# Summing one more half vector on VectorE, in its pauses, in a two-layer encoder kernel

## The reference, cut to what matters

```python
cs = silu(c)                                    # one vector of 1024
for i in range(2):
    mod = cs @ w_mod[i] + b_mod[i]              # 6 vectors of 1024: shift, scale, gate, twice
    sh_m, sc_m, g_m, sh_f, sc_f, g_f = split(mod, 6)
    h = rmsnorm(x) * (1 + sc_m) + sh_m          # x is 256 x 1024
    if i == 0:                                  # q, kv, index q, index k, u, v = split(h @ w_in)
        a = sparse attention with 8 heads, 64 keys chosen for each query
        u, v = gelu(u), layernorm(gelu(v))
        b = u * (w_s @ v + b_s)                 # w_s block lower triangular, 128 x 128 per group
        y = concat(a, b) @ w_o
    else:
        y = four trailing window means, minus h, times a small matrix per group
    x = x + g_m * y
    h = rmsnorm(x) * (1 + sc_f) + sh_f
    x = x + g_f * (32 experts, 2 chosen per token; each 1024 -> 256 -> 1024, SwiGLU)
out = rmsnorm(x)
```

## Time and profile before

| | |
|---|---|
| median of 3 runs | 684.23 us (683.09 to 684.79) |
| profiled execution | 683.93 us; its span from first to last instruction 682.1 us |
| TensorE busy | 625.4 us, 92% of the span |
| VectorE, ScalarE, GpSimd busy | 358.6, 179.3, 62.2 us |
| moved | 269.63 MB, 395 GB/s over the span |

### The profile page before, as it was taken

The page is one execution under the profiler, slowest core; times in us unless marked ns, Lnnn a source line. Parts: engine busy times, 40 slices in busy tenths (PEclk is TensorE's granted clock), DMA queues, the critical chain, the costliest instruction groups (busy, mean ns, idle before and its releaser), DMA issues.

```text
span 682.1 us, 11449 instructions
## 1 busy us (share of the span) xinstructions
PE 625.4 (92%) x4226; PEld 376.8 (55%) x4226; DVE 358.6 (53%) x869; ACT 179.3 (26%) x370; POOL 62.2 (9%) x111
## 2 busy tenths in 40 slices
PE   2799999999999999999999989999999999999894
PEld 1497758446665455545554457666555554555442
DVE  2258988998454643344334465735444344433445
ACT  2023352013432232122212233342223112321213
POOL 5010408950000000000000000000000000000000
PEclk9899999999999999999999999999999999999998
DMA  8999987999999999999999999999999999999991
GB/s 324 358 382 395 379 302 259 408 417 415 386 411 421 420 421 422 422 421 420 422 421 422 409 399 412 420 420 420 420 421 420 422 421 422 423 422 420 422 398 69
DMA packets 51534, 269.63 MB, mean 395 GB/s; under 512 B 4112, under 2 KB 6224, under 8 KB 27440
## 3 DMA queue, kind: packets, MB, share of 16 engines
q1 hardware_dynamic: 50720, 268.22, 97.0%
q0 software_dynamic: 784, 1.01, 0.5%
HBM read 268.17 MB, written 1.05 MB: 395 GB/s over the span
## 4 chain that ended last, share of the span: by engine, by line
PE 67%; DMA 19%; DVE 11%; issue 1%; ACT 1%; SPq 0%; POOL 0%; DVEq 0%; POOLq 0%
PE bank L965 15%; PE bank L977 14%; PE bank L998 12%; DMA ring<-in_w_gate 11%; DMA ring<-in_w_mod 8%; PE bank L1024 7%; PE bank L687 4%; DVE gates L1445 3%; PE bank L930 2%; PE bank L771 2%; DVE hT L1763 2%; PE bank L600 1%; PE bank L985 1%; PE bank L1081 1%; PE bank L734 1%
## 5 line engine op out<-in xcount | busy, mean ns | idle before, releaser
L965 PE MATMUL bank<-ring,arena 128*64 128x256 f32 x1024 | 116.8, 380 | 2.6 <-DMA ring<-in_w_gate 2.6
L977 PE MATMUL bank<-ring,arena 128*64 128x256 f32 x1024 | 117.2, 381 | 0.0
L965 PEld LDWEIGHTS bank<-ring,arena 128*64 128x64 f32 x1024 | 75.4, 137 | 50.9 <-issue 20.4
L977 PEld LDWEIGHTS bank<-ring,arena 128*64 128x64 f32 x1024 | 72.3, 137 | 41.2 <-issue 8.6
L1763 DVE SCALAR_TENSOR_TENSOR hT<-hT,bank 128x256 f32<-128x256 f32 x32 | 19.2, 601 | 136.6 <-PE bank L977 136.6
L1292 ACT CAST xn_parts<-arena 128x512 fp32r<-128x512 f32 x64 | 39.6, 619 | 106.8 <-DVE arena L1788 106.8
L1788 DVE SCALAR_TENSOR_TENSOR arena<-bank,hT,gates 128x512 f32<-128x512 f32 x64 | 48.0, 750 | 36.7 <-PE bank L998 35.4
L1024 PE MATMUL bank<-xn_parts,sel 128*128 128x512 f32 x256 | 67.1, 405 | 0.0
L998 PE MATMUL bank<-dn_w,hT 128*64 128x512 f32 x256 | 58.5, 598 | 1.1 <-ACT gates L1102 1.1
L1024 PEld LDWEIGHTS bank<-xn_parts,sel 128*128 128x128 f32 x256 | 45.7, 188 | 20.9 <-issue 12.4
L998 PE MATMUL bank<-gates,arena 128*64 128x512 f32 x112 | 51.1, 598 | 0.0
(11 more groups left out here) (324 smaller groups left out, 762.2 us busy)
## 6 DMA issues: line engine op xcount, KB each, us to landing
ring<-in_w_gate SPq DMA_DIRECT2D x32, 2048.0 KB, 17.7
ring<-in_w_up SPq DMA_DIRECT2D x32, 2048.0 KB, 18.3
ring<-in_w_mod SPq DMA_DIRECT2D x20, 2048.0 KB, 17.6
dn_w<-in_w_down SPq DMA_DIRECT2D x16, 2048.0 KB, 17.7
xn<-in_w_down SPq DMA_DIRECT2D x14, 1024.0 KB, 17.0
gates<-in_w_down SPq DMA_DIRECT2D x14, 1024.0 KB, 19.2
ring<-in_w_in SPq DMA_DIRECT2D x2, 2048.0 KB, 22.9
dn_w<-in_w_mod SPq DMA_DIRECT2D x2, 2048.0 KB, 12.0
```

Source lines behind the costliest of these rows:

```text
L965: ins = pe.matmul(bank[2][h * WIN:(h + 1) * WIN, 0:FE], xw[:, b, h, k, :], w[:, h, 0, k, :], start=(k == 0), stop=(k == KT - 1))
L977: ins = pe.matmul(bank[3][h * WIN:(h + 1) * WIN, 0:FE], xw[:, b, h, k, :], w[:, h, 1, k, :], start=(k == 0), stop=(k == KT - 1))
```

## The change

It has these parts.

1. `m4a` is summed by VectorE, no longer by TensorE: one slab after the attention's `divide`, the others at three points of `gelu_v`; `m4b` then adds onto that sum.
2. The gelu's polynomial takes one instruction, since ScalarE's square now carries the factor. The normalization of v goes from VectorE to ScalarE (`ln_bias`), and so does VectorE's copy of the sums over values (`keep_heads`), for both token tiles; the counter `cat_dve` is gone.
3. Rooms: `m5a` goes to ATT, `m5b` to ring 1; `usq` moves from dn_w to the arena (where q stood). m5a is issued when all attention weights are turned and v's layernorm has its mean square (`ln_ms`); before, m5b waited there for `bT_ready` too.
4. The distances' absolute value and the zeroing in w_s go from VectorE to GpSimd, early; w_s is turned on TensorE before the indexer's scores, and copied by ScalarE in two parts.
5. `reduce((0, 4))` stands before the output projection, `reduce((0, 3))` before its second half (before, both stood inside the second half).
6. The last early half, `("mod", 3)`, comes as two transfers of 1 MB, and TensorE takes its first two slabs when the first has come. The transfer of c is issued behind x's first tile.

```diff
-        gtmp, usq = scratch[:, 2048:3072]..., scratch[:, 3072:4096].rearrange("p (t d) -> p t d", t=4)
+        gtmp, usq = scratch[:, 2048:3072]..., ar(2048, 1024, t=4)
...
-                 ... (m3a, 2), (m3b, 0), (m5a, 1), (n4b, 2), (m5b, ATT),
+                 ... (m3a, 2), (m3b, 0), (m5a, ATT), (n4b, 2), (m5b, 1),
...
-        by_dve = [m2a, m2b, m4b, m3a, m3b, n4b, m5a, m5b]
+        by_dve = [m2a, m2b, m4a, m4b, m3a, m3b, n4b, m5a, m5b]
...
+                    if plan[n] == LAST_MOD:
+                        sp.dma_start(mod_at(n)[:, 0:2], src[:, 0:2]).then_inc(S["last_mod"], 16)
+                        sp.dma_start(mod_at(n)[:, 2:4], src[:, 2:4]).then_inc(arrived, 16)
...
-                if slot_of(n) in (ARENA_A, ARENA_B) or plan[n] == m5b:
+                if plan[n] == m5a:
+                    sp.wait_ge(S["p_turned"], 6)
+                    sp.wait_ge(S["ln_ms"], 1)
+                if slot_of(n) in (ARENA_A, ARENA_B):
...
             turn_p(0)
             turn_p(1)
-            vector((0, 4), (0,))
             pe.wait_ge(S["v_kept"], 2)
...
             values(1)
-            pe.wait_ge(S["cat_act"], 2)
-            pe.wait_ge(S["cat_dve"], 2)
+            reduce((0, 4))
+            pe.wait_ge(S["cat_act"], 4)
...
             def keep_heads(t):                     # ScalarE
-                act.wait_ge(S["pv_done"], 2 * t + 1)
-                act.copy(catT[0:HD, 0:4, t * P:(t + 1) * P], bank[3][0:HD, :]...)
+                act.wait_ge(S["pv_done"], 2 * t + 2)
+                for b in range(2):
+                    at = slice(b * HD, (b + 1) * HD)
+                    act.copy(catT[at, 0:4, t * P:(t + 1) * P], bank[3 + b][at, :]...)
...
             def gelu_poly(sq, v, after):           # VectorE
-                done(ts(sq, sq, GELU_A, 1.0, ALU.mult, ALU.add))
-                tt(sq, sq, v, ALU.mult).then_inc(after, 1)
+                stt(sq, sq, 1.0, v, ALU.add, ALU.mult).then_inc(after, 1)
...
+            accumulate((0, 4), 0, (0,))
             gelu_v()
-            keep_heads(0)
+            accumulate((0, 4), 0, (3,))
             accumulate((0, 4), 1)
```

More of the change, by code:

```diff
@@ L181, in trunk @@
                  (m2a, 0), (m2b, 1), (n0a, 2), (("in", "q"), ATT), (("in", "v"), 3), (n0b, 0), (("in", "u"), 1),
-                 (("out", 0), EARLY_W), (m4a, 2), (m4b, 0), (("out", 1), 3), (m3a, 2), (m3b, 0), (m5a, 1), (n4b, 2), (m5b, ATT),
+                 (("out", 0), EARLY_W), (m4a, 2), (m4b, 0), (("out", 1), 3), (m3a, 2), (m3b, 0), (m5a, ATT), (n4b, 2), (m5b, 1),
                  (n1a, ARENA_A), (n1b, ARENA_B), (n4a, ATT)]
@@ L193, in trunk @@
         chunk_no = {key: n for n, key in enumerate(by_pe)}
+        LAST_MOD = ("mod", 3)
         chunk_dmas = [2 if key == ("in", "kv") else 1 for key in plan]
@@ L387, in _ @@
                     chunk(place[n4a])
-                    sp.wait_ge(S["dve_used"], by_dve.index(m5a) + 1)
+                    sp.wait_ge(S["dve_used"], by_dve.index(m5b) + 1)
                     sp.wait_ge(S["chunk_done"], chunk_no["out", 1] + 1)
@@ L577, in vector @@
                     key = halves(vec)[part]
-                    arrived(key)
+                    if key == LAST_MOD:
+                        pe.wait_ge(S["last_mod"], 16)
+                    else:
+                        arrived(key)
                     w = mod_at(place[key])
@@ L598, in vector @@
                             k = part * 4 + kk
+                            if key == LAST_MOD and kk == 2:
+                                arrived(key)
                             for q in range(4):
@@ L738, in head_units @@
                                 ins.then_inc(done, 1)
+            pe.wait_ge(S["small_in"], 16 * SMALL)
+            pe.wait_ge(S["consts"], 2)
+            pe.wait_ge(S["col_turned"], 2)
+            for g in range(4):
+                ins = pe.transpose(bank[1][:, g * P:(g + 1) * P], ws_raw[:, g, :], ident[:])
+            ins.then_inc(S["ws_turned"], 1)
             pe.wait_ge(S["kiT_ready"], 1)
@@ L844, in _ @@
                         pe.wait_ge(S["bT_ready"], 1)
-                    if half == 1 and (part, t) == (0, 1):
-                        reduce((0, 4)), reduce((0, 3))
+                    if half == 1 and (part, t) == (0, 0):
+                        reduce((0, 3))
                     for k in range(4 * part, 4 * part + 4):
@@ L1227, in _ @@
             act.activation(flat(gtmp), flat(gtmp), ACT.Tanh, scale=GELU_C).then_inc(S["v_tanh"], 1)
-            keep_heads(0), keep_column((1, 0)), keep_u(0), keep_p(2), keep_p(3), keep_p(4), keep_p(5), keep_u(1)
+            keep_heads(0), keep_column((1, 0))
+            act.wait_ge(S["ln_bias"], 1)
+            for t in range(TT):
+                ins = act.activation(vtk[:, t, :], vtk[:, t, :], ACT.Identity, scale=stat[:, 18 + t:19 + t], bias=stat[:, 16 + t:17 + t])
+            ins.then_inc(S["vln_ready"], 1)
+            keep_u(0), keep_p(2), keep_p(3), keep_p(4), keep_p(5), keep_u(1)
             keep_heads(1)
@@ L1435, in accumulate @@
                     done(ts(acc, rows[:, :], ident[:, r:r + 1], None, ALU.mult))
-                elif part == 0:
+                elif part == 0 and vec != (0, 4):
                     dve.wait_ge(S["bias_kept"], ((0, 3), (0, 5)).index(vec) + 1)
@@ L1441, in accumulate @@
                     w = mod_at(place[key])[:, kk, :]
-                    if kk == 0 and part == 1 and halves(vec)[0] in by_pe:
+                    if kk == 0 and (part == 1 and halves(vec)[0] in by_pe or part == 0 and vec == (0, 4)):
                         ins = ts(acc, w, cs[:, 2, k:k + 1], None, ALU.mult)
```

65 lines of the change are left out of this document (30 added, 35 removed).

## The result

The changed kernel took 687.65 us (median; 686.15 to 692.33, 17 executions), the kernel before 685.31 in the same series (682.84 to 689.57, 17). The ratio is 1.0039 [1.0021, 1.0058]: 0.4% slower, where 683.6 was forecast and 685.4 was the upper end of the range. Of the 4.0 us between forecast and result, 1.1 lie in the starting point: the forecast counted from three executions of the kernel before with a median of 684.23, and 17 have 685.31.

A forecast was written before the change was run, and what follows sets the result against it. Bound: when TensorE reaches its first expert pass, set by VectorE's row up to the last residual. Terms -0.7 - 0.5 + 1.6 = +0.4 at `bT_ready`, less n4b's 0.76 wait: -0.4 to -0.5 from 683.93; predicted 683.6, range 681.3 to 685.4.

The forecast's parts named there:

- I take 0.7: At mod 3's matmuls: starting half of them before the second transfer lands gains 0.7 us, bounds 0 and 0.99.
- 0.5 us, not 1.9: At values(0): without m4a on TensorE it comes 0.5 us sooner, since ScalarE's copies of turned weights end at 97.52.
- VectorE's own work is paid: VectorE's row: m4a adds 4.7 us, mostly in pauses or offset by removed steps; m4b ends 0.9 us sooner.
- The GpSimd rival: GpSimd building layer 1's bands beside a busier VectorE: contention costs 1 us at most, 684.7; chance 0.03.
- is there at 112.9: m3a's landing: issued at 105.1 into an empty queue, it takes 7.8 us; VectorE waits 0.9 us.
- the cover is 1.4 us: After m3a's slabs: u's polynomial ends at 119.4, and the next item needs 120.8.
- point of decision: m3a's landing: once after 114.3 (112.9 + 1.4), each microsecond moves `bT_ready` and all behind it.
- slower by m3a: Rival: m3a, held by m4a's last slab, lands 2.6 us beyond the cover, giving 686.3; chance 0.10.
- Now ScalarE does both copies after both sums ... 4.9 us: Behind values(1): copies in a row, tanh and two products put `bT_ready` 4.9 us later, where it was 3.3.
- The n4b wait goes: After m3b on VectorE: the 0.76 us wait for n4b disappears, so n4b starts 0.4 to 0.5 us sooner.
- the rest follows one to one: Behind n4b: VectorE's work keeps its length; the loop's first gate load comes 0.4 us sooner, later times follow.
- The clock rival: Behind values(0): TensorE's 1.3 us pause lowers the clock, u's first half loses 1.7 us, 685.4; chance 0.05.

The follow-up runs named there:

- e6: The kernel before with only mod 3 split into two transfers of 1 MB, c first: 686.46 us, ratio 1.0022.
- e11: Changed kernel, c first, mod 3 in one transfer, m4a on TensorE, values(1) copies shared, slabs of m4b and m3b moved into VectorE's pauses: 683.2 us.
- e10: Changed kernel, c first, mod 3 in one transfer, values(1) copies shared, m4a's last slab ahead of the normalization's two steps: 684.98 us.
- e12: Whole changed kernel with two edits: values(1) copies shared by ScalarE and VectorE, m4a's last slab ahead of the normalization's two steps: 685.69 us.
- e7: Changed kernel with c first, mod 3 in one transfer, and m4a summed by TensorE again: 687.57 us.
- e1: The kernel before, unchanged, timed against itself: 684.88 us, ratio 0.9983.

## Why the prediction was wrong

Two things failed: the opening, where the cost of the late c was left out and the gain of the split did not come, and m3a's landing, which came 20.0 us behind w_o's second half where 18.1 was forecast and 19.5 was the latest that would have cost nothing. The terms in order of time, then the rivals:

- **The step that failed first in time is the one that isn't in the sum: c's transfer behind x's first tile.** It was named in front as part 6 and never priced, that is, taken at 0 without a reason. Its price is 0.8 +- 0.5 us by the fit at an equal clock, and the first half matrix lands 1.4 us later in the mean. That c's small packets now share the queues with x and the matrices fits the window at 4 us, but is argued, not shown.
- **"I take 0.7" for the split: 0** (-0.1 +- 0.5 at an equal clock). The lower bound, 0, was right, but for another reason than the one given: not a later second transfer, but TensorE, which in e6 is busy until both are there. The 0.99 was half of the 32 matmuls, in a profile where TensorE had waited 1.0 us for the transfer; in the other seven profiles without the split this wait was 0 to 1.2 us.
- **m4a off TensorE, "0.5 us, not 1.9": right.** values(1) ends 0.4 us sooner, 24.95 behind w_o's second half for 25.40.
- **"VectorE's own work is paid": mis-sized.** m3a went out 0.5 us later than worked out (10.8 behind w_o's second half, 10.3 forecast). One of the slabs lay beside GpSimd's step for the layernorm, which took 1.68 us for 0.71, so the pause stayed 0.68 us long although 1.27 us of work had been put into it. The GpSimd rival had the contention right and the place wrong. It cited the Trainium skill (GPSIMD Engine Reference, Specifications) for a way into SBUF shared with VectorE: the trace agrees, for the step took 1.68 in all six profiles with a slab of m4a beside it and 0.71 in all eight without one (e11 among them, which has slabs at the other places). No run takes that slab away alone.
- **m3a "is there at 112.9", 7.8 us behind its issue, "the cover is 1.4 us": wrong by one price.** It landed after 9.2 us. The 7.8 was that of w_o's second half, which takes 7.8 to 8.1 in all 14 profiles; m3a took 8.8 to 9.2 wherever it was issued 10.8 us behind w_o (four kernels), and 7.7 to 7.8 where 9.6 (e10, e12). The queue was empty at the issue in all of these. Two windows of the changed kernel narrow it:

```profile
108.14:114.14 6.00, 6.00 (x45) 5.65 (x44) 5.85 (x5) 3.40 (x7) 5.60 (x8) 1.00 0.81 291
115.00:116.00 1.00, 1.00 (x6) 0.89 (x5) 0.46 (x2) 0.00 (x0) 0.88 (x3) 1.00 0.89 254
```

and two of e10:

```profile
105.56:111.56 6.00, 6.00 (x46) 5.64 (x45) 5.82 (x7) 4.52 (x8) 5.60 (x8) 1.00 0.83 295
112.50:113.50 1.00, 1.00 (x7) 0.87 (x6) 0.73 (x3) 0.00 (x0) 0.87 (x4) 1.00 0.97 176
```

Six microseconds after the issue 1.75 and 1.77 MB had moved, so the extra microsecond lies in the last 0.35 MB, when m3b and m5a were in the queue too. The stream slows for a microsecond or two in both kernels (254 and 176 GB/s); why that delays m3a in the one and not in the other stays open. The forecast's own point of decision was a landing 19.5 us behind w_o's second half (114.3 in its count); it was 20.0. So the rival *slower by m3a*, given 0.10, is half of what happened, at a smaller price, since the copies held the tanh nearly as long.
- **"Now ScalarE does both copies after both sums ... 4.9 us": right.** With m3a in time (e7) it was 4.8. That it was seen and priced, and the wait beside it under-sized, is why neither undone alone shows anything: 123.49 and 123.92 are the two ends.
- **The n4b wait goes, and the rest follows one to one: right.** From `bT_ready` to residual 3 it was 27.8 us, 27.6 forecast. The loop's first gate load moved 2.80 us, the span 2.6.
- **The clock rival: did not come behind values(0)** (TensorE stood idle 1.36 us there, the granted clock stayed at 1.00, and u's first half took its full-speed 7.07). Clock stretches do decide much of each execution's time, in kernels with and without the change. Whether the changed kernel draws more of them (0.987 for 0.990) stays open. e12, which has its opening and most of its middle, has 0.992, which speaks against; the other five kernels with the split have the lowest five, which speaks for.
- **The chances** don't add up as written: 0.55 with the clock's 0.05 and GpSimd's 0.03 is 0.63, not 0.60. This changes nothing in the verdict.

The sum: forecast -0.45; c late +0.8, the split's 0.7 not had, and 0.7 in the middle (58.1 for the 57.5 that the forecast comes to) make +1.7, measured +1.3 +- 0.6 at an equal clock. The starting point (1.1) and the lower clock (1.2) make the rest of the distance from 683.6 to 687.65.

## What to carry to other kernels

Where two waits end at the same instruction, undoing either shows nothing; undo both before calling one harmless (57.9, 58.0, then 56.1). When work is moved to the engine whose row sets the stage, count its idle time and not its slabs, and ask which transfer its last slab releases: one slab ahead of two small steps was worth 1.4 us. Price every edit in the diff, the one-line move of a small transfer too. And look at a second profile of the same program before counting from the first: here the only one at hand lacked a stretch that 13 others have.

## What the runs showed of the hardware

- The same program scatters by 9 us (682.8 to 691.6 for the kernel before), with the granted clock from 0.997 to 0.979; stretches at 0.50 cost 1.7 us in the kv projection (5.65 us in one profile, 7.33 in 13), and up to 4 us in layer 0's routing (26.8 us from residual 3 to the first gate load in the profile before, 30.8 in e1).
- A transfer of 2 MB issued into an empty queue landed after 7.7 to 9.2 us, so an issue only just in time isn't in time.
- GpSimd's step on 128x2 took 0.71 us in the eight profiles where VectorE had no slab beside it, 1.68 in the six with a 128x1024 slab with two inputs.
